# One layer of a hybrid decoder: in-place bank additions in the FFN, and one weight sum of each unit made by an accumulating DMA

## The reference

```python
def swiglu(hn, w_gate, w_up, w_down):
    return (jax.nn.silu(hn @ w_gate) * (hn @ w_up)) @ w_down
hp = rms_norm(y_p, g_ffn_pre[l])
y_p = y_p + rms_norm(swiglu(hp, w_gate[l], w_up[l], w_down[l]), g_ffn_post[l])
```

## Time and profile before

| | |
|---|---|
| median of 3 runs | 981.15 us (977.53 to 982.27) |
| profiled execution | 976.96 us, its span 974.9 us |
| PE busy | 905.5 us (93%) |
| DVE busy | 670.0 us (69%) |
| ACT busy | 451.5 us (46%) |
| POOL busy | 231.0 us (24%) |
| units 1 to 27 on PE | about 597 to 921 us |
| PE waiting for others there | 29.3 us |

### The profile page before, as it was taken

How to read it: one execution, slowest core, us unless ns; L and a number is a source line. 1 busy time by engine, 2 the same in 40 slices (tenths; PEclk the granted TensorE clock), 3 DMA queues, 4 the chain that set the end, 5 groups by cost and what they waited for, 6 DMA issues and landing times.

```text
span 974.9 us, 17838 instructions
## 1 busy us (share of the span) xinstructions
PE 905.5 (93%) x7198; PEld 831.4 (85%) x7198; DVE 670.0 (69%) x1263; ACT 451.5 (46%) x831; POOL 231.0 (24%) x163
## 2 busy tenths in 40 slices
PE   4999999889999999999999998798999898999997
PEld 4999998656799889966489898798999898999997
DVE  4799974565443994123534878999669999769765
ACT  5553215665453571155335544454555444345442
POOL 3000001103000133100110023443454344545540
PEclk9999999999999999999999898999999999999999
DMA  8222207421522469095312005222322222222232
GB/s 231 92 88 85 84 2 251 152 94 47 199 66 87 136 209 345 2 347 215 120 55 87 1 2 178 80 81 72 115 88 87 87 87 87 87 87 87 98 124 92
DMA packets 81554, 110.55 MB, mean 113 GB/s; under 512 B 9505, under 2 KB 64674, under 8 KB 81090
## 3 DMA queue, kind: packets, MB, share of 16 engines
q1 hardware_dynamic: 81248, 109.37, 33.8%
q10 hardware_dynamic: 226, 0.05, 0.0%
HBM read 100.48 MB, written 8.93 MB: 112 GB/s over the span
## 4 chain that ended last, share of the span: by engine, by line
PE 68%; DVE 21%; issue 5%; ACT 4%; DMA 1%; SPq 0%; DVEq 0%; POOL 0%; ACTq 0%
PE pall L2301 20%; PE pall L2877 14%; PE pall L2313 6%; PE pall L2655 4%; PE pall L2338 4%; PE pall L2886 4%; DVE g_part_f L1406 2%; DVE ring_lo L1412 2%; DVE g_part L1412 2%; DVE g_part_f L1412 2%; DVE pall L1409 2%; PE pall L2706 1%; PE pall L2325 1%; PE pall L2371 1%; DVE w_sum L1412 1%
## 5 line engine op out<-in xcount | busy, mean ns | idle before, releaser
L817 POOL TENSOR_TENSOR ring_lo<-w_raw,ring_hi 128x512 fp32r<-128x512 f32 (+1 forms) x128 | 170.7, 1349 | 282.7 <-ACT ring_hi L1271 282.6
L2877 PE MATMUL pall<-x_hi,ring_hi 128*128 128x272 f32 x304 | 91.1, 300 | 20.0 <-DVE tt L1409 11.7
L2877 PE MATMUL pall<-x_sum,ring_hi 128*128 128x272 f32 x456 | 89.2, 292 | 6.5 <-ACT sq L1299 4.3
L2877 PE MATMUL pall<-x_lo,ring_hi 128*128 128x272 f32 x304 | 90.4, 297 | 0.0
L2877 PE MATMUL pall<-x_hi,ring_lo 128*128 128x272 f32 x304 | 90.3, 297 | 0.0
L2877 PE MATMUL pall<-g_part,ring_hi 128*128 128x272 f32 x448 | 85.9, 291 | 2.8 <-DVE z_down L1409 2.8
L1271 ACT ACTIVATE ring_hi<-w_raw 128x512 fp32r<-128x512 f32 (+1 forms) x128 | 75.5, 612 | 25.6 <-PE pall L2877 16.3
L2877 PEld LDWEIGHTS pall<-x_sum,ring_hi 128*128 128x128 f32 x456 | 72.8, 191 | 7.4 <-ACT sq L1299 4.5
L2877 PEld LDWEIGHTS pall<-x_hi,ring_hi 128*128 128x128 f32 x304 | 59.7, 197 | 21.9 <-DVE tt L1409 12.8
L2877 PEld LDWEIGHTS pall<-g_part,ring_hi 128*128 128x128 f32 x448 | 71.3, 191 | 3.6 <-DVE z_down L1409 3.6
L2301 PE MATMUL pall<-x_hi,w_hi 128*128 128x272 f32 x352 | 73.5, 290 | 0.5 <-issue 0.5
(11 more groups left out here) (460 smaller groups left out, 2399.6 us busy)
## 6 DMA issues: line engine op xcount, KB each, us to landing
w_raw<-in_w_gate SPq DMA_DIRECT2D x10, 1024.0 KB, 5.3
w_raw<-in_w_up SPq DMA_DIRECT2D x10, 1024.0 KB, 5.2
w_raw<-in_w_in SPq DMA_DIRECT2D x8, 1024.0 KB, 5.7
w_raw<-in_w_down SPq DMA_DIRECT2D x8, 1024.0 KB, 5.0
dm_kv<-in_cache_mem_v SPq DMA_DIRECT2D x5, 1024.0 KB, 14.1
w_raw<-in_w_out SPq DMA_DIRECT2D x4, 1024.0 KB, 9.2
d_k<-in_cache_k SPq DMA_DIRECT2D x16, 256.0 KB, 3.0
d_v<-in_cache_v SPq DMA_DIRECT2D x16, 256.0 KB, 4.0
```

What stands on the lines that cost most here:

```text
L817: e.tensor_tensor(w_part(ring_lo[:, q % RING, :], n), sev_source(n, i), w_part(ring_hi[:, q % RING, :], n).bitcast(F32), ALU.subtract)\
L2877: ins = mm(out, w, x, start=i in SEV_FIRST and j == 0 and s_, stop=j == np_ - 1 and t_, skip_group_check=i not in SEV_FIRST)
```

## The change

First, three additions in `sev_evac` of gate and up units write their sum into the PSUM bank that they read (`B_`, `C_`) in place of the SBUF tile, and what follows reads the bank. Second, s1 of units 2 to 27 is no longer made by VectorE. SP loads a21 a second time, straight into a buffer for s1 in SBUF, behind the load of the unit; GpSimd, when it has done its four low parts of unit n, issues a DMA that adds a22 from DRAM onto the s1 of unit n + 1. VectorE's s2 and ScalarE's high part 1 wait for this DMA. With that s1 stands in SBUF, s2 in bank 7 and s4 in bank 6. A few counts and semaphores are renamed to fit.

```diff
     def w_sums(n):
-        first = (bank(6), bank(7)) if sums_in_banks(n) else (w_sum[:, 0, :], w_sum[:, 1, :])
-        return [w_part(t, n) for t in (*first, w_sum[:, 2, :])]
+        if not sums_in_banks(n):
+            return [w_part(w_sum[:, i, :], n) for i in range(3)]
+        return [w_part(t, n) for t in (s1_second[:] if n == 2 else w_sum[:, n % 2, :], bank(7), bank(6))]
...
             e.dma_start(w_raw[:, sev_slot(n), 0:2 * np_ * 256].rearrange("p (k c) -> p k c", k=2 * np_), src).then_inc(w_loaded[sev_slot(n)], 16)
+            if sums_in_banks(n):
+                if n == 3:
+                    e.wait_ge(S("sum_lo"), 3)
+                elif n > 3:
+                    e.wait_ge(*low_ready(n - 2, 1))
+                e.dma_start(w_sums(n)[0], quarter_in_dram(n, 0, 1)).then_inc(S(f"x_in{n % 2}"), 16)
...
         for n in range(len(sev)):
             for i in (0, 3, 4, 6):
                 sev_lo(7 * n + i)
+            if sums_in_banks(n + 1):
+                e.wait_ge(S(f"x_in{(n + 1) % 2}"), 16 + 16 * ((n + 1) // 2))
+                e.dma_start(w_sums(n + 1)[0], quarter_in_dram(n + 1, 1, 1), accum_op=ALU.add).then_inc(S(f"s1_sum{(n + 1) % 2}"), 16)
...
-                e.wait_ge(S("w_sum"), 4 * sevens(n) + made[i])
+                if sums_in_banks(n) and i == 1:
+                    e.wait_ge(S(f"s1_sum{n % 2}"), 16 * (n // 2))
+                else:
...
-                add(s1, a21, a22).then_inc(S("w_sum"), 1)
-                e.wait_ge(S("w_sum"), 4 * sevens(n) + 1)
+                if n == 1:
+                    add(s1, a21, a22).then_inc(S("w_sum"), 1)
+                    e.wait_ge(S("w_sum"), 1)
                 sub(a21, a21, a11).then_inc(S("w_sum"), 1)
             if 2 in which:
...
+                if sums_in_banks(n):
+                    e.wait_ge(S(f"s1_sum{n % 2}"), 16 * (n // 2))
                 sub(s2, s1, a11).then_inc(S("w_sum"), 1)
...
             ended(3)
-            add(u0[:, H0], u0[:, H0], B_).then_inc(out, 1)
+            add(B_ if in_bank else u0[:, H0], u0[:, H0], B_).then_inc(out, 1)
...
-                mul(b11, u0[:, H0], g0[:, H0])
+                mul(b11, B_, g0[:, H0])
...
+                e.wait_ge(out, 4 * n + 1)
+                mul(u0[:, H0], B_, rstd[:, H0])
...
-            add(u0[:, H1], u0[:, H1], C_).then_inc(out, 1)
+            add(C_ if in_bank else u0[:, H1], u0[:, H1], C_).then_inc(out, 1)
             if what == "gate":
                 e.wait_ge(out, 4 * n + 3)
-                mul(u0, u0, rstd[:]).then_inc(S("gate_r"), 1)
+                mul(u0[:, H1], C_, rstd[:, H1]).then_inc(S("gate_r"), 1)
...
-                    done(mul(u0[:, H1], u0[:, H1], g0[:, H1]))
-                    g_sums(p)
+                    done(mul(C_, C_, g0[:, H1]))
+                    g_sums(p, C_)
```

More of the change, by code:

```diff
@@ L241, in build @@
     w_sum = at("w_sum", [P, 3, 512], F32, C0 + 87040)
+    s1_second = at("s1_second", [P, 512], F32, C0 + 50304)
     x_sum = at("x_sum", [P, 3, 2, 4, HALF], F32R, C0 + 60928)
@@ L366, in w_sums, with sums_made, quarter_in_dram @@
     def w_sums(n):
-        first = (bank(6), bank(7)) if sums_in_banks(n) else (w_sum[:, 0, :], w_sum[:, 1, :])
-        return [w_part(t, n) for t in (*first, w_sum[:, 2, :])]
+        if not sums_in_banks(n):
+            return [w_part(w_sum[:, i, :], n) for i in range(3)]
+        return [w_part(t, n) for t in (s1_second[:] if n == 2 else w_sum[:, n % 2, :], bank(7), bank(6))]
+    def sums_made(n):
+        return sum((3 if sums_in_banks(x) else 4) for x in range(n) if not classic(x))
+    def quarter_in_dram(n, k, m):
+        what, at_, np_ = sev[n]
+        w = A["w_down" if what == "down" else "w_gate" if what == "gate" else "w_up"][0].rearrange("(k p) c -> p k c", p=P)
+        if what == "down":
+            k0, c0 = 2 * GROUP * at_[0], at_[1] * 256
+        else:
+            k0, c0 = 0, at_ * 256
+        return w[:, k0 + k:k0 + 2 * np_:2, c0 + m * P:c0 + (m + 1) * P]
     def low_ready(n, i):
@@ L729, in _ @@
             if n >= 2:
-                e.wait_ge(S("w_sum"), 4 * sevens(n - 1)) if sevens(n - 1) else None
+                if sums_made(n - 1):
+                    e.wait_ge(S("w_sum"), sums_made(n - 1))
             if what == "down":
@@ L1219, in split_hi_first @@
             e.wait_ge(S("wx_in"), 32)
-            e.activation(wx_hi[s_][:], wx_raw[:, s_, :], ACT.Copy).then_inc(S("wx_hi"), 1)
+            e.activation(wx_hi[s_][:], wx_raw[:, s_, :], ACT.Copy).then_inc(S("y1_hi"), 1)
         def gained_half(a, k):
@@ L1266, in sev_hi @@
             if i in (1, 2, 4, 5) and not classic(n):
-                made = (None, 3, 4, None, 2, 4) if sums_in_banks(n) else (None, 1, 3, None, 2, 4)
-                e.wait_ge(S("w_sum"), 4 * sevens(n) + made[i])
+                if sums_in_banks(n) and i == 1:
+                    e.wait_ge(S(f"s1_sum{n % 2}"), 16 * (n // 2))
+                else:
+                    made = (None, None, 3, None, 1, 3) if sums_in_banks(n) else (None, 1, 3, None, 2, 4)
+                    e.wait_ge(S("w_sum"), sums_made(n) + made[i])
             else:
@@ L1916, in split_lo_first @@
         def split_lo_first(s_):
-            e.wait_ge(S("wx_hi"), s_ + 1)
-            sub(wx_lo[:, s_, :], wx_raw[:, s_, :], wx_hi[s_][:].bitcast(F32)).then_inc(S("wx_lo"), 1)
+            e.wait_ge(S("y1_hi"), SF + s_ + 1)
+            sub(wx_lo[:, s_, :], wx_raw[:, s_, :], wx_hi[s_][:].bitcast(F32)).then_inc(S("y1_lo"), 1)
         def add_half(i):
@@ L2016, in weight_sums @@
                 e.wait_ge(w_loaded[sev_slot(n)], 16 * ((U_FFN + n) // 2 + 1))
-                if n > 1:
-                    e.wait_ge(*low_ready(n - 1, 1))
                 if n == 2:
                     e.wait_ge(acc_out, J_FFN + 8)
-                add(s1, a21, a22).then_inc(S("w_sum"), 1)
-                e.wait_ge(S("w_sum"), 4 * sevens(n) + 1)
+                if n == 1:
+                    add(s1, a21, a22).then_inc(S("w_sum"), 1)
+                    e.wait_ge(S("w_sum"), 1)
                 sub(a21, a21, a11).then_inc(S("w_sum"), 1)
@@ L2027, in weight_sums @@
                     e.wait_ge(*low_ready(n - 1, 5))
+                if sums_in_banks(n):
+                    e.wait_ge(S(f"s1_sum{n % 2}"), 16 * (n // 2))
                 sub(s2, s1, a11).then_inc(S("w_sum"), 1)
-                e.wait_ge(S("w_sum"), 4 * sevens(n) + 3)
+                e.wait_ge(S("w_sum"), sums_made(n + 1) - 1)
                 sub(s4, a12, s2).then_inc(S("w_sum"), 1)
@@ L2064, in input_low, with g_sums @@
                 sub(x_sum[:, t, 1], input_made(t), x_sum[:, t, 0].bitcast(F32)).then_inc(S("x_sum_lo"), 1)
-        def g_sums(p):
+        def g_sums(p, b12):
             b11, b22, t1, t2, t3, t4, b21 = (g_part_f[:, p % GROUP, 7 + i, :] for i in range(7))
-            b12 = sq[:, 0, H1]
             sub(t3, b12, b22)
@@ L2099, in first_pair @@
             e.memset(small[:, 61:62], 0.0).then_inc(S("g_made"), 1)
-            g_sums(0)
+            g_sums(0, sq[:, 0, H1])
             e.memset(small[:, 61:62], 0.0).then_inc(S("g_made"), 1)
@@ L2132, in sev_evac @@
                 return
+            in_bank = what != "down"
             ended(3)
-            add(u0[:, H0], u0[:, H0], B_).then_inc(out, 1)
+            add(B_ if in_bank else u0[:, H0], u0[:, H0], B_).then_inc(out, 1)
             ended(4)
@@ L2155, in sev_evac @@
                 if plain(p):
-                    mul(g_part_f[:, p % GROUP, 9, :], u0[:, H1], g0[:, H1]).then_inc(S("g_made"), 1)
+                    mul(g_part_f[:, p % GROUP, 9, :], C_, g0[:, H1]).then_inc(S("g_made"), 1)
                 else:
-                    done(mul(u0[:, H1], u0[:, H1], g0[:, H1]))
-                    g_sums(p)
+                    done(mul(C_, C_, g0[:, H1]))
+                    g_sums(p, C_)
                     e.memset(small[:, 61:62], 0.0).then_inc(S("g_made"), 1)
@@ L2821, in during_first @@
             return at_k
-        e.wait_ge(S("wx_lo"), 2)
+        e.wait_ge(S("y1_lo"), SF + 2)
         for i in range(8):
```

## The result

The changed kernel takes 1062.55 us (median of 4 runs, 1060.57 to 1065.91), against 981.71 for the kernel before in the same series: ratio 1.084, 95% interval 1.079 to 1.088. It is 81 us slower, where 967 us was forecast. The profiled execution has a span of 1059.4 us, against 974.9 before.

A forecast was written before the change was run, and what follows sets the result against it. DVE bounds gate and up pairs, PE the down units. At L = 4.7, -19.6 (pairs) + 2.0 (down units) + 3.0 (last pairs) = -14.6 us from 981.15 gives 967 us; 8-in-10 range 952 to 1007.

The forecast's parts named there:

- L: Time from the end of GpSimd's low part 6 of one unit to the landing of the next unit's s1; taken as 4.7 us.
- upper end of 7.0: Largest L: the DMA lands wholly behind the 1024 KB load, at twice its own flow, 7.0 us.
- my middle: L between 3.85 us (engines shared half and half) and 5.55 (doubled traffic also shared); 4.7 taken.
- the full gain: Rival: L up to 4.1, the wait covered everywhere, 27 us gained, 954 us; chance 0.13.
- The loop: Rival: L above 5.5, the DMA waits on itself through DVE, ACT and GpSimd; 1000 to 1026 us; chance 0.38.
- 2L + 13.1: Shortest gate and up pair in us: two landings plus 7.1 in the up unit and 6.0 in the gate unit.
- the forecast's sum: Gains of seven pairs less losses of down units and two last pairs, as a function of L; -14.6 us at 4.7.
- second-group down units: Four down units that already stall 0.20 us; said to lose 4 x (L - 4.2), 2.0 us in the sum.
- DVE's savings: Work removed from DVE in gate and up pairs: 4.0 us a pair, from 25.3 to 21.3; 28 us over seven.
- The fourth rival: GpSimd's descriptor writing slows DVE's two-SBUF-input operations, taking half the 4.0 us a pair; 972 us; counted within the forecast's 0.35.
- SP's second load: Extra 256 KB load behind each unit's load; said to be hidden, with some 3 us left.
- The clock: PE's clock, 0.93 in the gate and up stretch; no term, since a slower PE costs nothing while DVE sets the pace.

The follow-up runs named there:

- e5: Changed kernel with a plain DMA from GpSimd in place of the accumulating one, same place, addition left out: 1010.86 us, ratio 1.033.
- e6: Changed kernel with SP holding back the 1024 KB load and the 256 KB load behind it until the accumulating DMA has landed: 977.45 us, ratio 1.000.
- e4: Changed kernel with the accumulating DMA replaced by SP's plain load of a22 ahead of the 1024 KB load, addition left out: 956.14 us, ratio 0.976.
- e10: Changed kernel with all three evacuation additions of second-group down units ahead of s2 in DVE's queue: 1054.05 us, ratio 1.078.
- e1: Kernel before with the in-place bank additions alone; s1 still made by VectorE, no new DMA: 967.02 us, ratio 0.986.
- e3: Changed kernel with three s1 buffers in place of two, the same DMAs issued one unit earlier: 964.01 us, ratio 0.983.
- e7: Changed kernel with the accumulating DMA issued behind GpSimd's low part 4 in place of 6, before the 1024 KB load: 956.89 us, ratio 0.978.
- e8: e3 with s1 of units 2 and 3 made by VectorE as before: 956.50 us, ratio 0.977.

## Why the prediction was wrong, point by point

- **The step that failed is the size of L:** "I take the middle, 4.7". It measured 7.9, and even the upper end of 7.0 was too low. The rows of before price a transfer by its bytes on shared DMA engines, and two things had a price in no row there. Accumulating costs 2.1 us beyond a plain load from the same queue, beside the 1024 KB load (e5). The company of that load costs 3.3 us (e6), against the 0.85 to 2.55 that I allowed for sharing and the second read together. Alone the DMA takes 4.6 us, already more than the 3.85 of my middle's lower end. The 3.0 us of the lowest end hold for what they were read from, a plain load by SP (3.1 in e4, and 956.14 us, the full gain's time). A plain load by GpSimd alone was not run, so how much of the 4.6 is GpSimd's path and how much the addition is open.
- **The rule that I set beside it.** The Trainium skill, DMA: Bandwidth & Descriptors, on the anatomy of one DMA on the GpSimd path, gives an estimate of 2.6 us; the runs have 5.8 for a plain one in company and 4.6 for an accumulating one alone, so they decide against its use here. The two source reads of the Trainium skill, Collectives: The Full Stack, on the bandwidth ceiling, point the right way (5.8 to 7.9). The 5.55 that I had worked out for doubled traffic is 2.4 us short all the same.
- **The loop was right.** It was named as the rival with 0.38. A pair should take 2L + 13.1: 28.9 at L = 7.9, measured 29.5; 24.7 at e5's 5.8, measured 25.4; 22.3 at e6's 4.6, measured 23.3. The constant is 0.6 to 1.0 us low. Put into the forecast's sum, L = 7.9 gives +25 for the pairs, +15 and +12 for the down units of the second and first group and +16 for the last pairs: +68 of the 81.
- **A second step failed:** that the second-group down units lose only what their stall takes. Two additions stand behind s2 in DVE's queue, and PE's pieces and so the ring wait for them: 3.7 us a unit more, 4 units (e10). With it the sum is 83, near the 84.5 us by which the profiled spans differ. Single stretches fit less well: three pairs, from the issue of 747.06 to that of 835.71, lost 14.5 us (88.65, against 74.16 before), where the sum has 10.8. A part of the agreement is chance.
- **The sum at the forecast's own L** was not tried cleanly. e6 has L = 4.6, for which the sum gives 964 us, and took 977.45; but it also loads its weights later.
- **DVE's savings** were 4.0 us a pair on paper. The loop hid them in the changed kernel; in e1 2.7 became 1.8, and in e3, where all count, 4.0 became 3.1 (a pair of 22.2, not 21.3). The fourth rival was so partly right: the slowness moved, to the low parts among others. But e1 has no DMA from GpSimd at all, so there it was not its descriptor writing. (That rival's "7 x 2.0 - 5 = -9" has its sign turned; a gain of 14 less a loss of 5 gives the -9.)
- **What was hidden as forecast:** SP's second load; it rose to 6.5 to 6.8 us beside the others and nobody waited for it, except GpSimd in e7, by up to 1.0 us, and in e6, by up to 0.4. The clock: 0.80 between 850 and 900, with PE busy 36.89 of 50 us. It is 1.00 again in e8, where the stalls are gone, so it follows them. Whether it lengthened the four slow units was not tried apart; PE's busy time there differs by some 1 us a unit between the changed kernel and e10.
- **The weighing.** I gave my middle 0.35 against 0.38 for the loop, and told the time of the group of cases with gains. With the landing unknown by 3.0 to 7.0 and the cover used up at 4.2 to 4.9, most of that interval lay on the losing side. The 52 us between e5 and the changed kernel show what such an unknown is worth when it is paid once a unit.

## What to carry to other kernels

Where an engine issues a DMA behind the work of one unit, and its own next unit depends on that landing, the unit can't be shorter than the landing plus the rest of the loop, whatever the engines' busy shares; issue it a unit earlier into one more buffer (e3, e8), or ahead of the large transfer that the same event releases (e7). When offloading an addition to an accumulating DMA, put a large number on its latency until it is measured, and ask what multiplies it: here 25 units. When operations with two SBUF inputs are slow, count on a part of the slowness moving to those that stay.

## What the runs showed of the hardware that I had not expected

- 256 KB from DRAM onto SBUF with an addition: 528 packets, 4.6 us alone, 7.9 us beside a 1024 KB load issued at the same moment; without the addition: 80 packets and 5.8 us beside that load (e5). From SP the same plain load is 528 packets and lands in 3.1 us when it is issued 0.4 us ahead of the large one (e4).
- Beside the accumulating transfer the large load lost 0.2 us (5.3 to 5.5), beside the plain one 1.0 (to 6.3): the accumulating one pays for nearly all of the sharing, the plain one does not.
- Issued 2.7 us ahead of the large load the accumulating transfer lands in 4.7 us, as if alone, and the large one in 6.6 (e7).
- GpSimd is busy 1.28 us with issuing an accumulating DMA and 0.76 us with a plain one of the same shape.
- Taking operations with two SBUF inputs away made others of that kind on VectorE slower, 1155 to 1333 ns and 915 to 1143 (e1).
